# Three-part fp32 matmuls on one core: a recurrent head's sums and spreads as 32-row pieces side by side, and three steps placed anew

## The reference, cut to what matters

```python
h = num / jnp.maximum(jnp.abs(den), jnp.exp(-m_t))[..., None]
...
hm = hm * lax.rsqrt(jnp.mean(hm * hm, axis=-1, keepdims=True) + EPS)
...
od_b = rmsnorm_2(od_b, subln_g[l]) * (1.0 - lam_init)
...
x = x + jnp.concatenate([mix_out, mem_out], axis=-1) @ w_out
```

## Time and profile before

| what | value |
|---|---|
| median of 3 runs | 1838.75 us (1837.64 to 1839.1) |
| the profiled execution's own time | 1836.94 us |
| its span, first to last instruction | 1835.2 us |
| PE (matmul) busy | 1815.8 us, 99% |
| VectorE busy | 935.6 us, 51% |
| ScalarE busy | 726.6 us, 40% |
| GpSimd busy | 272.4 us, 15% |
| TensorE in the chain that ended last | 93% |

### The profile page before, as it was taken

One profiled execution on the slowest core, in us unless ns is written; L12 is line 12 of the kernel. 1 busy time (PEld: TensorE's weight loads), 2 busy tenths in 40 slices (PEclk: granted clock), 3 DMA queues, 4 the chain that ended last, 5 costly groups with the idle time before them and its releaser, 6 DMA issues.

```text
span 1835.2 us, 21592 instructions
## 1 busy us (share of the span) xinstructions
PE 1815.8 (99%) x8853; PEld 1482.8 (81%) x8853; DVE 935.6 (51%) x1445; ACT 726.6 (40%) x1159; POOL 272.4 (15%) x241
## 2 busy tenths in 40 slices
PE   9999999999999999999999999999999999999998
PEld 7877788888888887787888888888876788888886
DVE  6877455442444456546543354458666443323324
ACT  5644444331332435654433133333566332222223
POOL 2001322210121200002221022003001222101210
PEclk9999999999999999999999999999999999999999
DMA  6121123222222332212222222232131223222221
GB/s 241 69 94 56 69 92 115 92 92 95 89 102 88 124 135 92 81 46 93 97 110 92 98 99 97 75 127 91 60 104 51 76 92 109 98 92 92 97 92 63
DMA packets 32338, 173.43 MB, mean 95 GB/s; under 512 B 4064, under 2 KB 6240, under 8 KB 14320
## 3 DMA queue, kind: packets, MB, share of 16 engines
q1 hardware_dynamic: 26848, 162.55, 24.7%
q10 hardware_dynamic: 5392, 9.51, 1.7%
HBM read 169.38 MB, written 2.13 MB: 93 GB/s over the span
## 4 chain that ended last, share of the span: by engine, by line
PE 93%; DVE 3%; ACT 2%; issue 0%; DMA 0%; POOL 0%; SPq 0%; ACTq 0%; DVEq 0%; POOLq 0%
PE ps L964 53%; PE ps L1239 19%; PE ps L898 7%; PE ps L983 6%; PE ps L1088 2%; PE ps L1133 2%; PE ps L1113 2%; DVE WL L1740 1%; PE ps L1172 1%; PE ps L1153 1%; DMA raw<-in_wall 0%; ACT PC L1476 0%; ACT WH L1315 0%; DVE hL L1708 0%; PE ps L878 0%
## 5 line engine op out<-in xcount | busy, mean ns | idle before, releaser
L964 PE MATMUL ps<-hH,WH 128*128 128x512 f32 x1456 | 571.4, 392 | 0.1
L964 PE MATMUL ps<-hH,WL 128*128 128x512 f32 x1456 | 566.8, 389 | 0.0
L964 PE MATMUL ps<-hL,WH 128*128 128x512 f32 x1456 | 566.7, 389 | 0.0
L1740 DVE TENSOR_TENSOR WL<-raw,WH 128x1024 fp32r<-128x1024 f32 (+2 forms) x308 | 377.3, 1264 | 352.0 <-ACT WH L1315 352.0
L1315 ACT ACTIVATE WH<-raw 128x1024 fp32r<-128x1024 f32 (+2 forms) x308 | 301.3, 1026 | 291.5 <-PE ps L1239 228.6
L964 PEld LDWEIGHTS ps<-hH,WH 128*128 128x128 f32 x1456 | 273.3, 188 | 64.4 <-issue 7.5
L964 PEld LDWEIGHTS ps<-hL,WH 128*128 128x128 f32 x1456 | 273.4, 188 | 57.4 <-issue 1.2
L964 PEld LDWEIGHTS ps<-hH,WL 128*128 128x128 f32 x1456 | 273.3, 188 | 57.1
L1239 PE MATMUL ps<-fL,WH 128*128 128x512 f32 x531 | 205.9, 388 | 0.0
L1239 PE MATMUL ps<-fH,WH 128*128 128x512 f32 x531 | 205.9, 388 | 0.0
L1239 PE MATMUL ps<-fH,WL 128*128 128x512 f32 x531 | 205.9, 388 | 0.0
(11 more groups left out here) (364 smaller groups left out, 1965.8 us busy)
## 6 DMA issues: line engine op xcount, KB each, us to landing
raw<-in_wall SPq DMA_DIRECT2D x140, 1024.0 KB, 4.6
raw<-in_wall SPq DMA_DIRECT2D x12, 768.0 KB, 4.0
bias<-in_bias ACTq DMA_DIRECT2D x12, 256.0 KB, 3.0
X<-in_xt SPq DMA_DIRECT2D x8, 256.0 KB, 9.1
CB<-rows ACTq DMA_DIRECT2D x8, 256.0 KB, 3.3
raw<-in_wall SPq DMA_DIRECT2D x4, 256.0 KB, 5.8
mrA<-in_memt ACTq DMA_DIRECT2D x4, 256.0 KB, 6.2
Mb<-m_rows ACTq DMA_DIRECT2D x4, 256.0 KB, 4.7
```

Source lines behind the costliest of these rows:

```text
L964: mm = e.matmul(ps[b][:, 0:N], ww[:, k, c:c + 128], x[:, k, 0:N], start=(k == 0 and i == 0), stop=(k == 7 and i == 2))
L1740: e.tensor_tensor(WL[n % NCV][:, c], raw[n % NRAW][:, c], WH[n % NCV][:, c].bitcast(F32), ALU.subtract).then_inc(*mark("wl", n, x))
```

## The change

1. `m_sums` on TensorE: the squares are now the moving side. Four fp32 matmuls with 32 columns of ones (L1193 of the new file) write 32 rows each of one bank: half a head's tokens (256) in each 32 rows. The factors stay in that shape, 128x256: the clamp, the root and the inverse are one instruction each on 128x256, and the eight diagonals are gone.
2. A new step `m_spread` on TensorE in the place of the matmuls of `m_norm`: per pair four fp32 matmuls of 32 rows and 256 columns with `pick`, the second half of the tokens behind a wait for the first of the same head.
3. `out_mid` for m = 0 to 3, in layers A, B and C.
4. The inverse of the differential heads' norm stands right behind the `probs` of pair 6; its root stays where it was.
5. The third store is cut in two.

```diff
--- before.py
+++ after.py
@@ -146,7 +146,7 @@
-STORES = ((0, 0, 2), (0, 2, 2), (0, 4, 4), (1, 0, 4), (1, 4, 2), (1, 6, 2))
+STORES = ((0, 0, 2), (0, 2, 2), (0, 4, 2), (0, 6, 2), (1, 0, 4), (1, 4, 2), (1, 6, 2))
 def order():
@@ -267,7 +267,7 @@
             between()
         tm(1, "mem" + name, "mv" + name, "mvcp", ntt=2)
-    def soft(stage, gens, per, before=None, between=None):
+    def soft(stage, gens, per, before=None, between=None, after_probs=None):
         us = SOFT[stage]
@@ -284,6 +284,8 @@
             if p < n:
                 for x in (0, 1):
                     put("probs", stage, p, x)
+            if after_probs:
+                after_probs(p)
             if early:
                 put("od_low", us[p - 2]["sink"][1])
             first, second = per(p)
@@ -319,7 +321,7 @@
     def out_rest(stage, nrm):
         m = 0
-        for x in (0, 1):
+        for x in range(4):
             put("out_mid", stage, x, *opened[x])
         while opened:
             n, c = opened.pop(0)
@@ -417,6 +419,7 @@
     fill(gens, 2)
     put("m_sums", 0)
     fill(gens, 1)
+    put("m_spread", 0)
     put("m_norm", 0)
     put("m_norm", 1)
     for hd in (2, 3):
@@ -434,6 +437,7 @@
     for t in range(3):
         put("gated", t)
     fill(gens, 1)
+    put("m_spread", 2)
     put("m_norm", 2)
     put("m_norm", 3)
     run_deferred()
@@ -507,9 +511,13 @@
     put("fence", "fox")
     gens.append(out_first("C"))
-    after_values = {(5, 1): [("od_two",)], (6, 0): [("od_all",)], (6, 1): [("od_mask",)],
+    after_values = {(5, 1): [("od_two",)], (6, 0): [("od_root",)], (6, 1): [("od_mask",)],
                     (7, 0): [("od_spread", 0, 1)], (7, 1): [("od_spread", 2, 3)]}
     places = []
+
+    def inverse(p):
+        if p == 6:
+            put("od_all")
     def between_C(p):
         places.append(p)
@@ -521,7 +529,7 @@
             put("cum", 2 * (p - 3) + 1)
     soft("C", gens, lambda p: {4: (1, 0), 5: (1, 0), 6: (1, 0), 7: (1, 0), 8: (1, 1), 9: (1, 1)}.get(p, (1, 1)),
-         None, between_C)
+         None, between_C, inverse)
     out_rest("C", "n2")
     rstd("n2", 61)
     ffn(2, "n2", None)
@@ -1181,15 +1189,26 @@
                         w.wait_ge(*at(*before))
                     for hd in (h0, h0 + 1):
                         w.wait_ge(*at("msqS", hd))
-                        sums(b, msq[hd % 2], 4 * (hd - h0), ("msums", hd))
-
-                elif what == "m_norm":
-                    hd = a[0]
-                    b, before = bank(("mf", hd), ("mnorm", hd, 1))
-                    if before:
-                        w.wait_ge(*at(*before))
-                    w.wait_ge(*at("mdiag", hd, 3))
-                    e.matmul(ps[b][:, :], ones, fac[hd % 2][:, :], start=True, stop=True).then_inc(*mark("mspread", hd))
+                    for g in range(4):
+                        mm = e.matmul(ps[b][32 * g:32 * g + 32, 0:256], ones[:, 0:32],
+                                      msq[g // 2][:, 256 * (g % 2):256 * (g % 2) + 256], start=True, stop=True)
+                    mm.then_inc(*mark("msums", h0))
+
+                elif what == "m_spread":
+
+                    h0 = a[0]
+                    for hd in (h0, h0 + 1):
+                        b, before = bank(("mf", hd), ("mnorm", hd, 1))
+                        if before:
+                            w.wait_ge(*at(*before))
+                    w.wait_ge(*at("mfac", h0, 1))
+                    for h in (0, 1):
+                        for x in (0, 1):
+                            if h:
+                                w.wait_ge(*at("mspread", h0 + x, 0))
+                            r = slice(64 * x + 32 * h, 64 * x + 32 * h + 32)
+                            e.matmul(ps[BANK[("mf", h0 + x)]][:, 256 * h:256 * h + 256], pick[r, :], fac[1][r, 0:256],
+                                     start=True, stop=True).then_inc(*mark("mspread", h0 + x, h))
                 elif what in ("out_first", "out_mid", "out_rest", "out_all"):
                     stage, m, n, c = a
@@ -1204,7 +1223,7 @@
                         out_part(stage, BANK[("out", stage, m)], n, c, seq[early:7], ("outb", stage, m))
                     elif what == "out_rest":
                         b = BANK[("out", stage, m)]
-                        out_part(stage, b, n, c, seq[7 if m < 2 else early:], ("out", stage, m))
+                        out_part(stage, b, n, c, seq[7:], ("out", stage, m))
                         turns.append(b)
                     else:
                         out_part(stage, b, n, c, list(range(8)), ("out", stage, m), True)
@@ -1428,7 +1447,7 @@
                         elif hd == 1:
                             w.wait_ge(*at("pv", "A", 1))
                         else:
-                            w.wait_ge(*at("msums", hd - 2))
+                            w.wait_ge(*at("msums", 0))
                         r = slice(64, 128) if hd % 2 == 0 else slice(0, 64)
                         e.dma_start(den[hd % 2][r, :], m_rows[4 + hd:5 + hd, :].broadcast_to([64, 512])).then_inc(
                             s_E[hd % 2], 16)
@@ -1527,9 +1546,8 @@
                 elif what == "m_sums":
                     h0 = a[0]
-                    c = 64 + 4 * h0
                     w.wait_ge(*at("mfac", h0, 0))
-                    e.activation(small[:, c + 16:c + 24], small[:, c:c + 8], ACT.Sqrt, scale=1.0 / 192).then_inc(
+                    e.activation(fac[0][:, 256:512], fac[0][:, 0:256], ACT.Sqrt, scale=1.0 / 192).then_inc(
                         *mark("mfacA", h0))
                 elif what == "gated":
@@ -1676,7 +1694,7 @@
                     e.activation(dq[:, hd, :], ps[BANK[("v", "C", i)]][:, :], ACT.Copy, scale=2.0 ** -40).then_inc(
                         *mark("odc", hd))
-                elif what == "od_all":
+                elif what == "od_root":
                     w.wait_ge(*at("odD", "r"))
                     e.activation(sq[1][:, :], sq[1][:, :], ACT.Sqrt, scale=0.64).then_inc(*mark("odq"))
@@ -2005,30 +2023,25 @@
                     w.wait_ge(*at("mnum", hd, 1))
                     e.scalar_tensor_tensor(out=D[rd, :], in0=p, scalar=-1.0, in1=D[rd, :], op0=ALU.mult,
                                            op1=ALU.max).then_inc(*mark("mden", hd, 1))
-                    w.wait_ge(*(at("msums", hd - 2) if hd >= 2 else at("pv", "A", 1)))
+                    w.wait_ge(*(at("msums", 0) if hd >= 2 else at("pv", "A", 1)))
                     e.tensor_tensor(D[r, :], q[r, t, :], q[r, t, :], ALU.mult).then_inc(*mark("msqD", hd))
                 elif what == "m_sums":
                     h0 = a[0]
-                    c = 64 + 4 * h0
-                    w.wait_ge(*at("msums", h0 + 1))
-                    e.tensor_scalar(small[:, c:c + 8], ps[BANK[("mq", h0)]][:, 0:8], 192e-34, 192e35, ALU.max,
+                    w.wait_ge(*at("msums", h0))
+                    if h0:
+                        w.wait_ge(*at("mfacA", 0))
+                    e.tensor_scalar(fac[0][:, 0:256], ps[BANK[("mq", h0)]][:, 0:256], 192e-34, 192e35, ALU.max,
                                     ALU.min).then_inc(*mark("mfac", h0, 0))
                     w.wait_ge(*at("mfacA", h0))
-                    e.reciprocal(small[:, c:c + 8], small[:, c + 16:c + 24]).then_inc(*mark("mfac", h0, 1))
-                    w.wait_ge(*at("mfac", h0, 1))
-                    for hd in (h0, h0 + 1):
-                        if hd >= 2:
-                            w.wait_ge(*at("mspread", hd - 2))
-                        for i in range(4):
-                            o = c + 4 * (hd - h0) + i
-                            e.tensor_scalar(fac[hd % 2][:, i * 128:i * 128 + 128], ident, small[:, o:o + 1], None,
-                                            ALU.mult).then_inc(*mark("mdiag", hd, i))
+                    if h0:
+                        w.wait_ge(*at("mspread", 1, 1))
+                    e.reciprocal(fac[1][:, 0:256], fac[0][:, 256:512]).then_inc(*mark("mfac", h0, 1))
                 elif what == "m_norm":
                     hd = a[0]
-                    w.wait_ge(*at("mspread", hd))
+                    w.wait_ge(*at("mspread", hd, 1))
                     w.wait_ge(*at("msqP", hd))
                     for n, (t, r, _) in enumerate(pieces(hd)):
                         e.scalar_tensor_tensor(out=q[r, t, :], in0=q[r, t, :], scalar=col("hg", t, p=r),
```

## The result

Fifteen runs of the changed kernel have a median of 1841.95 us (1840.09 to 1843.92), fifteen of the kernel before beside them 1838.37 us (1837.21 to 1839.10). The ratio is 1.0021, with a 95% interval of 1.0014 to 1.0029: the change costs 3.6 us, 0.2%. The profiled execution took 1843.92 us with a span of 1842.2 us, against 1836.94 and 1835.2 us, so it shows 7.0 us more, nearly twice the difference of the medians. Why one execution shows so much more is part of the answer. Two slow runs, 7548.82 us of the kernel before and 6448.88 us of kernel 11 (its profiled one), are left out of everything that follows.

A forecast was written before the change was run, and what follows sets the result against it. TensorE, busy 99% of the span, was taken as the bound. Terms -1.4 + 0.5 + 1.3 + 1.4 + 2.2 - 2.7 - 0.1 = +1.2 us gave a median of 1839.9 us, range 1835.5 to 1842.5 us.

The forecast's parts named there:

- Pair 2: Recurrent heads' sums and spreads, pair 2: factors ready in time, so the whole saving counts, -1.4 us.
- The rival in which the groups don't run side by side: Sums and spreads: column groups run one behind the other, sums save nothing, spreads take 2.1 us; 1842.7 us; chance 6%.
- the reading of the 128x1 sums by a fixed cost per instruction: Sums: by the skill's page the old 16 take 0.4 us, so new ones cost 0.16 us per pair.
- Pair 0: Sums and spreads, pair 0: VectorE is late, TensorE's wait grows from 0.5 to 2.6 us, +0.5 us.
- Seventh parts: Output products: six more matmuls ahead of m = 0's end make `WL` later; A +2.2, B +1.3, C +1.4 us.
- The rival in which they cost nothing: Output products: m = 4's weight unit is ready for another reason, 4.9 us drop out; 1835.0 us; chance 12%.
- Inverse: Differential norm, layer C: an earlier inverse shortens TensorE's 3.6 us wait for a ScalarE copy to 0.9 us, -2.7 us.
- The rival in which the stall stays: Layer C: the 3.6 us wait hangs on something else or `fkr` and `WL` pay; 1842.6 us; chance 8%.
- Store: End of kernel: the split third store closes a hole in DMA traffic, the fourth is no earlier; -0.1 us.
- Both of the forecast's marks for being wrong: TensorE's waits: wrong if those for `WL` total no more than 1.7 us, or C's wait stays over 3 us.

The follow-up runs named there:

- kernel 11: The changed kernel with thrown-away matmuls in all four of TensorE's waits of 2 us and more (pair 0, A, B, C): 1837.09 us.
- 5: The changed kernel with the seventh parts (`out_mid`, `out_rest`) put back as before: 1833.49 us.
- 10: Kernel 5 with the seventh parts of four tiles in layer B alone: 1837.23 us.
- kernel 1: The kernel before with only the inverse of the differential norm placed anew: 1832.34 us.
- 2: The kernel before with only `out_mid` for all four tiles: 1846.81 us.
- 4: The changed kernel with three thrown-away matmuls in TensorE's wait of pair 0: 1838.73 us.
- 6: Kernel 5 with pair 0's spread and norms one more step of other tiles later: 1829.44 us.
- 7: The kernel before with four thrown-away matmuls in TensorE's wait of layer C for the ScalarE copy: 1835.88 us.
- 3: The kernel before with only the new sums and spreads of the recurrent heads: 1839.33 us.

## Why the prediction was right, and where it was wrong

The time, 1841.95 us, lies in the range but 2.1 us over the forecast of 1839.9, and at +0.2% it stands on the border between no change and slower. The split of the 3.6 us: clean times +1.9 us, and the rest, 1.7 us, is clock (forecast nothing). Of the 1.9 us some 0.4 lie in the first 40 us and 0.5 in the last spread at the lower clock of the end; the terms of the forecast make up the other 0.9 us (forecast +1.2). The median of before holds 3.1 us of it over its clean time, that of after 4.9.

- **Pair 2, right to 0.1 us.** Sums 0.57 us (forecast 0.56), spread 1.42 (1.45), no wait: 3.40 us before, 1.99 now, -1.4. The rival in which the groups don't run side by side is refuted, and so is the reading of the 128x1 sums by a fixed cost per instruction: as the row said, they were worth 1.1 us. (This rival's price, 2.8 us, counted the spread's 0.27 us twice; by the forecast's own terms it is 2.4 us.)
- **Pair 0, the work right, the clock missing.** Clamp, root and inverse took 0.35, 0.42 and 1.76 us (0.36, 0.42, 1.68), the wait 2.7 us (2.6). Of the spread's later start, 1.7 us, 0.6 came from an earlier point: the clamp began at 163.70 instead of 163.11 us, and in kernels 5 and 10 at 163.30 and 163.17, so this varies between executions, with the first 40 us. At the upper clock the spread takes 1.46 us (5), 0.5 less than before; so +0.6 us, forecast +0.5. But the idle time "won in the sums" brought a lower stretch, up to 3.4 us.
- **Seventh parts, the waits right.** A 2.3 us (forecast 2.2), B and C 2.2 us each where they were 0.8 and 0.9 (1.4 more each; forecast 1.3 and 1.4): +5.1 us of waits to the forecast's +4.9. Behind them +1.6 us each in A and C by the clock. The rival in which they cost nothing is refuted.
- **Inverse, right, and worth more.** -3.3 us of wait in kernel 1 and in after alike (forecast -2.7): the two DMA issues also moved ahead, in after to 1396.55 and 1396.91 us, under other work of ScalarE. (Kernel 1's scores begin only 2.8 us earlier because TensorE has 0.7 us less done in its first 40 us.) The rival in which the stall stays is refuted: 0.3 us of it are left. Unpriced was the stretch behind the old wait, which went with it: 6.5 us in all by kernel 1's median.
- **Store.** From the first of the last adds (1833.86 us) to the end 8.34 us, 8.46 before: -0.1, as forecast. That add comes 0.5 us later behind the last spread, which takes 1.20 us instead of 0.68 since the lower clock of the end begins ahead of it.

**The step that failed** is the pricing of every wait at its own length. The forecast added up microseconds of waiting as if TensorE came out of each at full speed. The trace that it worked from had the counter-example: the 17 instructions of the two windows behind the wait in C stand at a granted clock of 0.69 and 0.50, and the 3.42 us of the earlier trace rows for ten matmuls of the scores after it (2.05 us for nine in after) went unquestioned. With 1.7 us behind each wait of 2 us and more, one gone and four come, the sum would have been 1.2 + 3 x 1.7 = 6.3 us; the profiled execution shows 7.0 us, the medians 3.6, since not each wait is punished each time. That the range held owes something to luck, two omissions of opposite sign: the stretch that went with C's old wait and the stretches behind the new ones. Both of the forecast's marks for being wrong (no wait for `WL` over 1.7 us in all; a wait over 3 us in C) looked at waits alone, and would not have caught this.

Why an execution loses 1.7, 3.4 us or nothing behind the same wait no run tested, but the profiles say much of it. The Trainium skill (TensorE: Matmul & The Clock Gate, What's actually happening) says that the gate's look at the engine's activity runs freely and isn't reset by a kernel. The traces agree: within each of the eight profiles that have such stretches, their starts and that of the last one at the end lie whole multiples of one and the same step apart, to 0.02 us (166.70, 252.03, 1446.70 and 1832.40 us in after; 248.90, 1399.20, 1450.40 and 1836.10 us in 2). Carry these points on, and the four waits for `WL` of 2.2 us without a stretch behind them (B in after and 2, B and C in 4) are just those that a point cuts with at least 0.3 us on either side; the seven with one lie between two points, to 0.2 us. So where a wait falls decides, and that moves with every microsecond ahead of it. What stays open: pair 0's wait is cut so in 5 and 10 too (1.8 and 0.9, 1.5 and 1.2 us) and a stretch came all the same, 2.5 and 2.2 us behind its end.

## What to carry to other kernels

On an engine that is busy 99% of the time, look at the granted clock behind each wait before adding up waits: here one of 2.2 to 3.9 us often cost up to 1.7 or 3.4 us more, and one of 1.5 us or less nothing. Work saved in front of a wait is not neutral but can be a loss, since it makes the idle time longer (pair 0); moving the waiting step behind other work takes away wait and stretch together (6, 4.05 us for a wait of 2.7), and where that can't be done, matmuls nobody needs in the wait give the clock back (4, 7, 11). When one profiled execution is further from another than the medians are, and single runs of a kernel come in steps, compare the times less what the clock took from a busy engine, and take out a stretch at the start that the change doesn't touch; those add up over the parts here to 0.2 us.

## What the runs showed of the hardware

- Stretches at the lower level (1.2 GHz) ahead of the end come in two sizes: 1.7 or 3.4 us lost, nothing between, in the 13 profiles (all but 11's). Three of them begin before the wait is over, up to 1.2 us; the others up to 2.5 us behind it. Kernels with none have runs within 0.4 to 1.0 us of each other; those with unfilled waits over 2 us scatter by 1.9 to 3.8 us.
- By the length of the wait ahead of them, over these profiles: 3.6 to 3.9 us in C, 3 of 3 were followed by a lower stretch; 2.7 us in pair 0, 4 of 4; 2.2 to 2.3 us for `WL`, 7 of 11 (A 3 of 3, B 2 of 5, C 2 of 3); up to 1.5 us, none. With matmuls in the wait none of 5.
- A 128x1 sum with its own 128 columns of weights costs 0.105 us; eight instructions with the squares as the moving side, in four column groups, took 0.57 us wherever read (after, kernels 3 to 6).
